# Starting the gate phases two chunks earlier, moving dot products, and cutting GpSimd's subtractions into pieces

## The reference

```python
q = jnp.einsum('td,de->te', xc, wq).reshape(PEER_CHUNK, PEER_HEADS, 2, PEER_QDIM // 2)
s = jnp.einsum('thpd,hpnd->thpn', q, sub_keys)
sv, si = lax.top_k(s, PEER_TOPK)                       # 16 of 128 keys, 8 heads, 2 sides
cand = (sv[:, :, 0, :, None] + sv[:, :, 1, None, :]).reshape(PEER_CHUNK, PEER_HEADS, -1)
cidx = (si[:, :, 0, :, None] * PEER_NKEYS + si[:, :, 1, None, :]).reshape(...)
top, pos = lax.top_k(cand, PEER_TOPK)                  # 16 experts of 16384 for a token and head
eidx = jnp.take_along_axis(cidx, pos, axis=-1)
g = jax.nn.softmax(top, axis=-1)
a = jax.nn.gelu(jnp.einsum('thkd,td->thk', u[eidx], xc), approximate=False)
return jnp.einsum('thk,thkd->td', (g * a), v[eidx])
```

## Time and profile before

| what | value |
|---|---|
| median of 3 runs | 1542.12 us (1541.91 to 1545.63) |
| the profiled execution | 1545.63 us |
| its span in the profile | 1543.8 us |
| TensorE (PE) busy | 1493.2 us, 97% |
| VectorE (DVE) busy | 1260.6 us, 82% |
| ScalarE (ACT) busy | 710.0 us, 46% |
| GpSimd (POOL) busy | 622.9 us, 40% |
| DMA | 417.14 MB, mean 270 GB/s |

### The profile page before, as it was taken

One profiled execution on the slowest core, in us unless ns is written; L12 is line 12 of the kernel. 1 busy time (PEld: TensorE's weight loads), 2 busy tenths in 40 slices (PEclk: granted clock), 3 DMA queues, 4 the chain that ended last, 5 costly groups with the idle time before them and its releaser, 6 DMA issues.

```text
span 1543.8 us, 24322 instructions
## 1 busy us (share of the span) xinstructions
PE 1493.2 (97%) x8276; PEld 1328.7 (86%) x8276; DVE 1260.6 (82%) x2476; ACT 710.0 (46%) x1403; POOL 622.9 (40%) x510
## 2 busy tenths in 40 slices
PE   5999999999999999999889999999999999999997
PEld 5877777888999999999889999999999988888886
DVE  5788665639999879988859888889899988888777
ACT  3444553232345657667444444444444434443433
POOL 1121300033451524344246565556677655555300
PEclk9999999999999999999999999999999999999999
DMA  9754320032354788989799999999999999999962
GB/s 365 272 171 163 136 83 1 32 106 93 100 177 153 267 265 263 298 264 319 244 357 387 348 359 359 355 361 355 389 394 386 356 382 411 384 380 390 344 243 96
DMA packets 164099, 417.14 MB, mean 270 GB/s; under 512 B 12697, under 2 KB 70169, under 8 KB 163873
## 3 DMA queue, kind: packets, MB, share of 16 engines
q1 hardware_dynamic: 95936, 244.88, 44.6%
q0 software_dynamic: 41472, 151.01, 26.0%
q10 hardware_dynamic: 26594, 20.05, 4.0%
HBM read 376.57 MB, written 38.80 MB: 269 GB/s over the span
## 4 chain that ended last, share of the span: by engine, by line
PE 81%; DVE 14%; ACT 2%; DMA 2%; issue 1%; ACTq 0%; SPq 0%; DVEq 0%
PE bank_S L1029 16%; PE bank_T L1029 11%; PE bank_G L1029 5%; PE bank_T L1007 5%; PE bank_O L969 5%; PE bank_O L971 5%; PE bank_O L970 5%; PE bank_S L969 3%; PE bank_S L971 3%; PE bank_S L970 3%; PE bank_O L755 2%; PE bank_S L722 2%; DVE mod_acc L2147 2%; DVE v_sb L2153 1%; DVE v_sb L2140 1%
## 5 line engine op out<-in xcount | busy, mean ns | idle before, releaser
L1628 ACT ACTIVATE v_hi<-v_raw 128x1024 fp32r<-128x1024 f32 x124 | 131.5, 1061 | 287.4 <-PE bank_G L1029 276.4
L1600 ACT ACTIVATE u_hi<-u_raw 128x1024 fp32r<-128x1024 f32 x128 | 135.4, 1058 | 217.9 <-PE bank_O L971 107.1
L2407 DVE TENSOR_TENSOR v_lo<-v_raw,v_hi 128x1024 fp32r<-128x1024 f32 x124 | 152.0, 1226 | 88.5 <-ACT v_hi L1628 62.2
L969 PE MATMUL bank_S<-h_hi,u_hi 128*128 128x352 f32 x576 | 196.5, 341 | 11.1 <-DVE h_lo L2240 3.5
L1361 POOL DMA_INDIRECT row<-in_peer_v,stage x128 | 176.9, 1382 | 42.2 <-issue 37.8
L1361 POOL DMA_INDIRECT row<-in_peer_u,stage x128 | 144.7, 1131 | 104.7 <-POOL stage L1357 99.1
L970 PE MATMUL bank_S<-h_lo,u_hi 128*128 128x352 f32 x576 | 186.6, 324 | 0.0
L2397 DVE SCALAR_TENSOR_TENSOR y<-row,wgt,y 128x1024 f32<-128x1024 f32 x128 | 164.4, 1284 | 0.0
L2423 DVE SCALAR_TENSOR_TENSOR row<-row,h 128x1024 f32<-128x1024 f32 x128 | 156.2, 1220 | 0.0
L969 PE MATMUL bank_O<-h_hi,u_hi 128*128 128x352 f32 x448 | 145.1, 324 | 0.0
L970 PE MATMUL bank_O<-h_lo,u_hi 128*128 128x352 f32 x448 | 144.3, 322 | 0.0
(11 more groups left out here) (426 smaller groups left out, 3927.3 us busy)
## 6 DMA issues: line engine op xcount, KB each, us to landing
u_raw<-in_u_t SPq DMA_DIRECT2D x128, 512.0 KB
v_raw<-in_peer_v SPq DMA_DIRECT2D x128, 512.0 KB
g_in<-gates SPq DMA_DIRECT2D x32, 768.0 KB
ada_late<-in_w_ada SPq DMA_DIRECT2D x8, 2048.0 KB, 8.3
gates<-g_out SPq DMA_DIRECT2D x8, 2048.0 KB, 10.2
spill<-a_act ACTq DMA_DIRECT2D x64, 176.0 KB
a_act<-spill SPq DMA_DIRECT2D x16, 704.0 KB
w_raw<-in_w_in SPq DMA_DIRECT2D x20, 512.0 KB, 3.7
```

Of the source, the lines that this page charges most:

```text
L969: pe.matmul(ps[:, 0:DX], u_hi[q][:, kk], h_hi[:, k, GT * P:S - XT], start=(k == 0), stop=False)
L1600: act.activation(u_hi[c % 2][:, :], u_raw[:, c % 2, :], ACT.Copy).then_inc(s_uhi, 1)
L1628: act.activation(v_hi_end[:, i % TAIL, :] if end else v_hi[:, c % 2, :], v_raw[c % 4][:, :], ACT.Copy)\
L2407: dve.tensor_tensor(lo[:, q, :], v_raw[c % 4][:, :], hi[:, q, :].bitcast(f32), ALU.subtract)\
```

## The change

1. `GAPS` goes from [25, 6, 6, 6] to [23, 7, 6, 6]. The first phase starts after 23 chunks instead of 25; the second and third and fourth each start one chunk earlier in the count (after chunks 36, 50 and 64 have been reached instead of 37, 51 and 65), and six chunks follow the last phase instead of five.
2. `FIRST_LOW` goes from 17 to 15: Pool subtracts 15 chunks ahead of the decoding, VectorE takes over two chunks sooner.
3. `DOTS_AFTER` moves with the chunk numbers, and in the fourth gap by one more: 3, 2 and 2 products stood after the second, third and fourth chunk of the gap; now they stand at the first, second and third.
4. `last_and_columns` transposes after half of the chunk instead of a quarter.
5. Pool's subtractions for `wq_lo` and for the chunks below `FIRST_LOW` are cut into four instructions of 128x256 each. The later ones stay whole.

```diff
-GAPS = [25, 6, 6, 6]
+GAPS = [23, 7, 6, 6]
...
-FIRST_LOW = 17
+FIRST_LOW = 15
...
-DOTS_AFTER = {32: 1, 33: 1, 34: 1, 46: 1, 47: 1, 48: 1, 60: 3, 61: 2, 62: 2}
+DOTS_AFTER = {30: 1, 31: 1, 32: 1, 45: 1, 46: 1, 47: 1, 58: 3, 59: 2, 60: 2}
...
-                a_chunk(last, last, range(KD // 4))
+                a_chunk(last, last, range(KD // 2))
...
-                a_chunk(last, last, range(KD // 4, KD))
+                a_chunk(last, last, range(KD // 2, KD))
...
-                pool.tensor_tensor(wq_lo[e % 2][:, :], wq_raw[:, e % 4, :], wq_hi_of(e)[:, :].bitcast(f32),
-                                   ALU.subtract).then_inc(s_qlo, 1)
+                for a in range(0, D, 256):
+                    part = slice(a, a + 256)
+                    ins = pool.tensor_tensor(wq_lo[e % 2][:, part], wq_raw[:, e % 4, part],
+                                             wq_hi_of(e)[:, part].bitcast(f32), ALU.subtract)
+                ins.then_inc(s_qlo, 1)
...
-                pool.tensor_tensor(u_lo[c % 2], by_k(u_raw[:, c % 2, :]), by_k(u_hi[c % 2][:, :]).bitcast(f32),
-                                   ALU.subtract).then_inc(s_ulo, 1)
+                for k in range(0, KD, 2 if i < FIRST_LOW else KD):
+                    part = slice(k, k + 2 if i < FIRST_LOW else KD)
+                    ins = pool.tensor_tensor(u_lo[c % 2][:, part, :], by_k(u_raw[:, c % 2, :])[:, part, :],
+                                             by_k(u_hi[c % 2][:, :])[:, part, :].bitcast(f32), ALU.subtract)
+                ins.then_inc(s_ulo, 1)
```

## The result

The change makes the kernel slower. It takes 1553.11 us (median of 4 runs, 1551.63 to 1553.72) against 1543.23 of the kernel before in the same comparison (4 runs, 1541.91 to 1545.63): a ratio of 1.0060, with an interval of 1.0043 to 1.0079, so some 9.3 us more. 1547.2 were forecast, with a range that ended at 1551.5. The profiled execution took 1552.52, with a span of 1550.7. The profiled execution of before (1545.63) lay 2.4 above its median, so the two traces show only 6.9 of the difference.

What follows compares the result with a forecast made beforehand. The prediction took the end of VectorE's `best16`, ahead of the decoding, to set the time up to the phases. Its terms, 7.8 - 1.0 + 0 + 2.8 - 2.5 - 2.0 = +5.1 us, gave 1547.2 us, range 1539.5 to 1551.5.

Steps and rivals of the forecast that it cites:

- slower still: Up to the decoding: Pool gets between all sums, TensorE's clock falls again; +10.7 us, 1552.8; chance 0.07.
- T: When VectorE ends `best16` and the decoding can start: 471.68 us before the change, 470.7 forecast.
- Step 2: VectorE's sums in `best16`: Pool's pieces let T come 1.0 us sooner, bounds -1.5 to 5.0.
- Step 3: Chunks 2 to 14: the pieces delay TensorE 2 to 5 us, costed at nothing because the later decoding covers it.
- Step 1: Ahead of the first phase: two chunks fewer, so TensorE wants the decoding sooner; costs 7.8 us minus what T gains.
- Step 4: Heads of phases one to three: transposes after half the chunk make TensorE wait; +2.8 us, bounds 0 and 3.5.
- Step 5: Fourth gap: products one chunk sooner remove TensorE's 2.50 us wait; gain 2.5 us, bounds 0 and 2.5.
- The clash: Before the fourth phase: Pool's subtraction holds up VectorE's instruction, TensorE waits 2.34 us; it stays; if gone, 2.3 more gained.
- Step 6: After the last phase: one chunk more covers waits put down to late loads; gain 2.0 us, between 0 and 3.2.

Runs made afterwards that it cites:

- the eight pieces: Kernel before with GpSimd's early subtractions cut into eight pieces of 128 columns, nothing else: 1550.54 us, 1.0045.
- PSUM: Kernel before with the first side's best values in a PSUM bank, so each sum has one SBUF input: 1541.76 us, 0.9988.

## Why the prediction was wrong

The sign and the main mechanism held: the time up to the phases is set by the decoding, and moving the phases up puts the loss there. The time lay outside the range, and of the four rivals the one that came nearest is "slower still", with its chance of 0.07 and its +10.7 us: T later (by 2.0, it had 1.5) and the half at its upper bound. By its steps:

**Step 2, T, failed, and its sign with it.** It took a gain of 1.0, with bounds from -1.5 to 5.0. Measured was a loss of 2.0 between the two profiles. Other kernels with whole subtractions have 132.66 and 132.69 or, where no group falls on GpSimd at 442 to 444 us, 132.05 to 132.09, against which it is 2.1 and 2.7. By time the pieces cost 3.7 us alone, and 2.6 to 3.8 in the changed kernel. The step had named the right mechanism as its lower bound, a piece between any two sums, and had the rows for it, and then took a value between the two. The lower bound was itself too small: it reckoned 0.3 more work per subtraction (measured 0.43), and not that longer work falls on more groups.

**Step 3, nothing for TensorE, held.** TensorE waits 3.1 us in all for GpSimd in chunks 2 to 14, against 1.6 before, so the pieces add 1.5, a little under the 2 to 5 us named as the price if the cover were gone; the wait of 6.89 behind them covers it.

**Step 1, 7.8 us, held by the profile.** Chunk 21 starts 33.25 us after T, with two chunks less done. The reason given for it was only partly right, though. I had taken T as what sets the waits of 2.28 and 0.66 in the kernel before. With T 4.8 us sooner, waits of 2.05 and 1.49 remain there. What sets them is the 29.0 us that VectorE takes from its first remainder to its seventh (29.0 as well in the changed kernel), for TensorE's 23.4. T counts only as far as it moves the first remainder: by 1.0 us in the kernel before, where the rounded rows of chunk 17 are not there earlier, and by all of it once the shift has TensorE come to the first remainder before VectorE does.

**Step 4, +2.8.** The trace shows 2.5 for the three heads (waits of 0.62 and 0.41, 0.59 and 0.97, 0.60 and 1.19 in the changed kernel, 4.4 in all, against 0.29, 0.52 and 1.09, 1.9 in all, before); the times show 3.4 in both kernels, which is the step's upper bound (3.5).

**Step 5, -2.5.** Measured -2.8, by time (the products alone) and by trace (0.29 and 2.50 gone). The clash is there in both kernels, as said, but its row was read as more than it is: GpSimd's subtraction was ahead of VectorE's instruction by 0.06 us. In the traces of the pieces, the eight pieces, the shift, the half and PSUM, each alone, all with the products where they were, GpSimd's subtraction begins later, no instruction of VectorE is held up there, and the phase's head waits 0.23 us or less.

**Step 6, -2.0.** The waits behind the last phase are 1.2 us (0.99, 0.22) against 4.1 (0.73, 2.47 and 0.94 before the main loop): -2.9, within its bounds with the 0.94 that the step had not counted. The reason given was the late loads, and it is not borne out: in the changed kernel ScalarE still waits for `u_raw` by 4.76 us (4.50 before) at 787.55. What took the waits away stays open.

**A term left out: the clock.** Two falls of TensorE's granted clock follow waits. The one behind the 6.89 (0.75 in 470 to 480) costs nothing, since chunk 21 comes no later after T. The one behind the 2.34 (0.83 in 760 to 770, 1.00 before) takes 10 x 0.17 = 1.7 us of TensorE's work, but most of that is covered: the changed kernel with whole subtractions has the same wait (2.32) and no fall (1.00 over 740 to 800), and from the fourth phase's first multiplication to the main loop it takes 44.88 us (803.57 - 758.69) against 45.29 (806.15 - 760.86), with 0.97 more of waiting at the phase's second group. So the fall costs 0.4 us. Only the slowest rival had a clock term, and it read the fall at 491.21 too short:

```profile
492.00:496.00 4.00, 4.00 (x17) 4.00 (x16) 3.83 (x7) 0.68 (x2) 0.00 (x0) 0.57 0.45 131
```

That is 4 x 0.43 = 1.7 us in the kernel before, not 0.9.

Set against the trace: 7.8 + 2.0 - 0.25 (33.25 for 33.5) + 2.5 - 2.8 - 2.9 + 0.4 = 6.75. The main loop starts 7.3 us later after the start of `best16` than before (806.15 - 337.97 against 799.82 - 338.92). So the sum of +5.1 was 2.2 us short in the trace: step 2 adds 3.0 to it and the clock 0.4, the other steps take 1.75 back (0.25, 0.3, 0.3 and 0.9), and 0.5 is left unexplained.

**The base.** The remaining 2.4 us between trace and time lie in the profiled execution of before. It had `best16` begin at 338.92 and take 132.76, where the trace of the kernel with the products alone has 337.31 and 132.09: 2.3 us by which that one execution was late ahead of the decoding. The start of `best16` lies anywhere from 337.25 to 339.47 in the fifteen traces, so this is scatter of single executions and not a cause. I set the sum against an execution from the slow end of the scatter (1541.57 to 1545.23 in 20 later runs). Its rows also had less waiting behind T, 3.3 us, than the trace of the kernel with the products alone, 4.6 (0.56, 2.29, 0.24 and 1.50).

**What stays open.** The single costs by time (shift 8.0, pieces 3.7, half 3.4, products -2.8) add up to 12.3, and the whole change costs 9.3. The 3 us are no more than the intervals of the five ratios allow; 2.0 of them are there already without the pieces (8.0 - 2.8 + 3.4 = 8.6 for 6.6 measured). The clock in 740 to 800 us differs between kernels (0.94 to 1.00) for no edit that I could name: in all traces each fall between 400 and 800 us stands in or right behind a wait of TensorE of 1.84 to 7.23 us, but in the kernel with the products alone three waits of 2.29 to 2.34 have none behind them (1.00 in 485 to 500 and in 740 to 800). That the shift still costs 3 to 4 us when T comes early follows from step 1. Chunk 21 starts 160.84 us after the start of `best16` in the kernel with shift, products and PSUM (498.49 - 337.65), chunk 23 in the one without the shift 165.25 (504.72 - 339.47): 4.4 us sooner with 7.8 less done, so 3.4 are lost. The first remainder on VectorE begins only 4.2 us sooner there (130.68 for 134.83), where the shift asks for 7.8.

## What to carry to other kernels

Before an engine's work is cut into pieces to let another through, look at what the other one issues: a run of short instructions takes turns with the pieces and waits for one ahead of each of its own, and only the longest single wait gets shorter, not the sum. To end such a clash, take one of the operands out of SBUF. And when an engine is to be made earlier, look at the first thing it hands over: the selection's end 4.8 us sooner moved the first remainder by 1.0 and was worth 1.8 us, 6.9 sooner moved it by 6.8 and was worth about 7, depending on which of the two engines came first to the meeting point.

## What the runs showed of the hardware that I had not expected

Sums of VectorE with both inputs in SBUF and GpSimd's subtractions alternate instruction by instruction even when VectorE's four sums are queued back to back: a group of four takes 2.04 us beside one GpSimd instruction of 2.39, 2.05 beside four of 0.74, and at most 1.76 beside eight of 0.46, of which it meets four. Cutting one GpSimd subtraction of 1024 columns costs 0.14 us for each further piece, half of the 0.28 that I had estimated from the Trainium skill (GPSIMD Engine Reference, "Elementwise — side-by-side cycle accounting").
